# HGRN mixer: the key-by-query products of levels 64 and 32 with stationary tiles of 64 and 32 columns

## Chip, cores and metric

One NeuronCore of a Trainium2 chip. The metric is the device time of one execution in microseconds (us), the median of several runs.

## The reference, cut to what matters

Four sequence-mixing layers follow each other on 512 tokens of 1024 features, in fp32, each with a feed-forward network behind it. The change touches the third, the HGRN mixer with 8 heads of 128 keys and 128 values. For token t and an earlier token s of one head,

```
forget = lower_bound + (1 - lower_bound) * sigmoid(f);  k = 1 - forget;  q = silu(q) / sqrt(128)
scores[t, s] = sum_k q[t, k] * k[s, k] * prod over j in (s, t] of forget[j, k]     (s <= t)
o[t] = sum_s scores[t, s] * v[s]
```

The decay depends on the key feature, so it can't be taken out of the sum over k. The reference walks through chunks of 32 tokens with a state; the kernel computes the same sums otherwise.

## The kernel before

**Weights.** Each 128x1024 slot of weights comes by DMA to `raw`, is rounded to `w_hi` by ScalarE (L1015) and gets its remainder `w_lo` from VectorE (`low_over`, L1492). A dense product is then three fp32r matmuls, L443, L444 and L445, of 128 stationary columns and 512 moving ones; one slot is 24 of them.

**The levels.** `cq` and `ck` hold queries and keys with the features on the partitions and 512 tokens along the free dimension. The scores are built by halving: level 0 has the diagonal, and level m (`LEVELS = (1, 2, 4, 8, 16, 32, 64)`, index `lv - 1`) has the pairs in which the key is in the first half and the query in the second half of the same block of 2m tokens. Between two levels VectorE multiplies queries of second halves (L1972), keys of first halves (L1973) and the products of forget gates (L1974) onward (`decay`). Longer distances than 128 tokens follow after the levels (L884, L888).

TensorE computes a level for four heads e (group g, head 4g + e), in banks 4 to 7 of PSUM. For each of `TT` = 4 tiles of 128 tokens there is one fp32 matmul, L855: all 128 keys of the tile are stationary, and the 64 queries of second halves move. It gives 128 keys x 64 queries, of which a level needs only some. VectorE takes these out with a mask (`keep_level`, L1950, `copy_predicated`): only entries whose key is in the first half of the query's own block are copied to `ca`; all others of the bank are left. The mask `cmask` comes from the host.

**Order of the work.** Each engine's program is written out by hand. TensorE does, in group 0, level 0, then a slot of the value projection, level 1, the next slot, and so on; level 32 (`lv` 6) stands between value slots 5 and 6, and level 64 (`lv` 7) behind value slots 6 and 7. In group 1 each level is followed by a slot of the gate projection: level 32, gate slot 6, level 64, gate slot 7. After level 64 come the products with the values (L872, which waits for `level_kept`, and in group 1 for `g_evac`), then L884, L896, L888 and L900. Each L855 group of a head waits for `upd` (the decays for this level, L846) and for `level_kept` of the level before, and its last matmul raises `level_full`.

VectorE does per level, head by head, `keep_level(g, lv - 1, e)` and `decay(g, lv, e)`; then, in group 1, the gate's evacuation (L1978) and more, and the weights' remainder L1492.

Each fp32 matmul of the program stands in the trace as two pairs of a weight load (PEld LDWEIGHTS) and a MATMUL: L855 has 256 matmuls and 512 pairs. "128*128", "128*64" and "128*32" in the rows are rows and columns of the array that an instruction takes. Two other places of the kernel already use column tiles: L959 and L716 (attention values, 64 columns at partitions 0 or 64, in turns), and L770 (the depthwise convolution, 32 columns at partitions 0, 32, 64 and 96). L716 has seven matmuls a head, three with 256 moving columns and four with 128.

Of the kernel before, what the change touches and what calls it, by code (L numbers as in the profile page):

```python
# [12 lines left out]
P = 128  # L13
# [14 lines left out]
LEVELS = (1, 2, 4, 8, 16, 32, 64)  # L28
# [98 lines left out]
def build(nc, weights, vectors, squares, select_d, masks_d, x_t, out_t):  # L127
    with ExitStack() as ctx:
        def sb(name, shape, dt, where=ctx):
            return where.enter_context(nc.sbuf_tensor(name, shape, dt))  # L130
# [60 lines left out]
        with ExitStack() as hgrn:  # L191
            with ExitStack() as qk:
                cq = sb("cq", [P, HG_HEADS, T], F32, qk)
                ck = sb("ck", [P, HG_HEADS, T], F32, qk)
# [26 lines left out]
        bank = [ctx.enter_context(nc.psum_tensor(f"bank{i}", [P, T], F32)) for i in range(8)]  # L221
# [218 lines left out]
        def _(pe):  # L440
            def product(out, wh, wl, xh, xl, start, stop):

                pe.matmul(out, wh, xh, start=start, stop=False)  # L443
                pe.matmul(out, wh, xl, start=False, stop=False)  # L444
                return pe.matmul(out, wl, xh, start=False, stop=stop)  # L445
# [234 lines left out]
            for k in range(KC):  # L680
                wide = [w[:, k, :, :].rearrange("p r n -> p (r n)") for w in (wf_hi, wf_lo)]
                last = product(bank[4][:, :], *wide, u_hi[:, k, :], u_lo[:, k, :], k == 0, k == KC - 1)
# [120 lines left out]
            def value_slot(n):  # L803
                def free(t):
                    if n == 0:
                        pe.wait_ge(c_evac, 2 * KC)
                    elif n == 4:
                        pe.wait_ge(i_evac, t + 1)
                token_major(SLOT["c_i"] + n, bank, n % 4, n % 4 == 3, free if n in (0, 4) else None)

            def gate_slot(n):
                if n < 2:
                    pe.wait_ge(co_evac, n + 1)
                else:
                    pe.wait_ge(g_evac, n - 1)
                chunk(SLOT["c_g"] + n, 0, bank[n % 2][:, :], u_hi, u_lo)

            def head_square(hd):

                pe.wait_ge(sq_ready, SQ["c_head"] + hd + 1)  # L820
                if hd < 4:
                    pe.wait_ge(co_evac, 4)
                    out = bank[2 + hd % 2]
                else:
                    pe.wait_ge(far_kept, 16)
                    out = bank[hd]
                if hd in (2, 3):
                    pe.wait_ge(rs_ln, RS["c_head"] + hd - 1)
                pe.matmul(out[:, :], ones[:, :], sq[:, hd % 2, :], start=True, stop=True).then_inc(sq_used, 1)
# [3 lines left out]
            for g in range(2):  # L833
                for lv in range(N_LEVEL):
                    last_first = g == 0 and lv == N_LEVEL - 1
                    if last_first:
                        value_slot(lv)
                    for e in range(4):
                        hd = 4 * g + e
                        if lv == 0:  # L840
                            pe.wait_ge(c_qkf, 3 * (hd + 1))
                            if g:
                                pe.wait_ge(far_kept, 8)
                        else:

                            pe.wait_ge(upd, upd_count(g, lv, e))  # L846
                            pe.wait_ge(level_kept, 4 * (N_LEVEL * g + lv - 1) + e + 1)
                        for t in range(TT):
                            s = slice(t * P, (t + 1) * P)
                            if lv == 0:  # L850
                                out, queries = bank[4 + e][:, s], cq[:, hd, s]
                            else:
                                out = bank[4 + e][:, t * P // 2:(t + 1) * P // 2]
                                queries = cq[:, hd, s].rearrange("p (b two s) -> p b two s", two=2, s=LEVELS[lv - 1])[:, :, 1, :]
                            last = pe.matmul(out, ck[:, hd, s], queries, start=True, stop=True)  # L855
                        last.then_inc(level_full, 1)
                    if g:
                        gate_slot(lv)
                    elif not last_first:
                        value_slot(lv)  # L860
                    if g and 1 <= lv <= 4:
                        head_square(lv - 1)

                for e in range(4):
                    hd = 4 * g + e
                    pe.wait_ge(level_kept, 4 * (N_LEVEL * g + N_LEVEL - 1) + e + 1)
                    if g == 0:
                        pe.wait_ge(i_evac, KC)
                    else:
                        pe.wait_ge(g_evac, KC)  # L870
                    for t in range(TT):
                        last = pe.matmul(bank[e][:, t * P:(t + 1) * P], cv[:, t, hd * P:(hd + 1) * P],  # L872
                                         ca[:, e, t * P:(t + 1) * P], start=(t == 0), stop=False, skip_group_check=True)
                    last.then_inc(pv_part, 1)

                for far in range(2):
                    for e in range(4):
                        hd = 4 * g + e
                        pe.wait_ge(upd, upd_count(g, N_LEVEL + far, e))
                        if far:  # L880
                            pe.wait_ge(far_kept, 8 * g + e + 1)
                        if far == 0:
                            for i in range(2):
                                last = pe.matmul(bank[4 + e][:, i * P:(i + 1) * P], ck[:, hd, 2 * i * P:(2 * i + 1) * P],  # L884
                                                 cq[:, hd, (2 * i + 1) * P:(2 * i + 2) * P], start=True, stop=True)
                        else:
                            for i in range(2):
                                last = pe.matmul(bank[4 + e][:, 2 * i * P:2 * (i + 1) * P], ck[:, hd, i * P:(i + 1) * P],  # L888
                                                 cq[:, hd, 2 * P:4 * P], start=True, stop=True)
                        last.then_inc(far_full, 1)  # L890
                    for e in range(4):
                        hd = 4 * g + e
                        pe.wait_ge(far_kept, 8 * g + 4 * far + e + 1)
                        for i in range(2):
                            if far == 0:
                                last = pe.matmul(bank[e][:, (2 * i + 1) * P:(2 * i + 2) * P],  # L896
                                                 cv[:, 2 * i, hd * P:(hd + 1) * P], ca[:, e, i * P:(i + 1) * P],
                                                 start=False, stop=False, skip_group_check=True)
                            else:
                                last = pe.matmul(bank[e][:, 2 * P:4 * P], cv[:, i, hd * P:(hd + 1) * P],  # L900
                                                 ca[:, e, 2 * i * P:2 * (i + 1) * P], start=False, stop=(i == 1),
                                                 skip_group_check=True)
                        last.then_inc(pv_part if far == 0 else co_full, 1)
# [68 lines left out]
            for t in range(TT):  # L972
                last = pe.transpose(bank[0][:, t * P:(t + 1) * P], ut[:, 1, t * P:(t + 1) * P], ident)
# [32 lines left out]
        def _(act):  # L1006
# [69 lines left out]
            def keep(stat, n, src, t):  # L1076

                _, gain, at, _ = BOUNDARY[stat]
                bias = shifted_gain[:, n:n + 1] if stat == "b_post" else 0.0
                act.activation(m[:, n, t], src, ACT.Identity, scale=col(gain, at + n), bias=bias).then_inc(made_ready, 1)  # L1080
# [21 lines left out]
            def half_input(stat, half, chunks):  # L1102

                made, _, _, split = BOUNDARY[stat]
                for c in chunks:
                    act.wait_ge(h_ready, RESID[made] + PAIRS * half + c // 2 + 1)
                    act.activation(u_hi[:, c, tokens(half)], h[:, c, tokens(half)], ACT.Identity, scale=pre_gain(split, c))\
                       .then_inc(uh_ready, 1)
# [1044 lines left out]
def upd_count(g, lv, e):  # L2153

    per_group = 4 + 8 * 12
    before = 0 if lv <= 1 else 4 + 12 * (lv - 2)
    return per_group * g + before + (e + 1 if lv == 1 else 3 * e + 2)
# [83 lines left out]
```

## Time and profile before

| | us |
|---|---|
| median of 3 runs (2430.32 to 2433.72) | 2433.08 |
| the profiled execution | 2434.33 |
| its span, first to last instruction | 2432.5 |

Times in rows are us from the span's start unless ns stands there. "PE" is the matmul part of TensorE and "PEld" its weight loads, which run beside it; DVE is VectorE, ACT ScalarE. Ends of matmuls are modelled. In rows of a timeline, xN says how many instructions of one kind were merged into the row, and a bracket at the end says how long the engine had been idle and what released it.

### The profile page before, as it was taken

The numbers are of one execution on the slowest core, as the hardware profiler recorded it, in microseconds if no ns is written. First come the engines' busy times: TensorE is split into PE (matmuls) and PEld (weight loads), VectorE is DVE, ScalarE is ACT, GpSimd is POOL, SyncE is SP. The second block draws the span as 40 slices with busy tenths as digits, with TensorE's granted clock in tenths as the row PEclk, the third lists the DMA queues.
The fourth block names the chain that finished last, engine by engine and source line by source line (L and its number), as shares of the span: only waits on it lengthen the run. The fifth ranks groups of instructions, "written<-read, shape, count | busy, mean of one in ns | idle before, by whom it ended". The sixth has DMA issues, their size and how long they took to land.

```text
span 2432.5 us, 32810 instructions
## 1 busy us (share of the span) xinstructions
PE 2364.1 (97%) x12314; PEld 1963.0 (81%) x12314; DVE 1313.0 (54%) x2017; ACT 866.8 (36%) x1314; POOL 23.9 (1%) x16
## 2 busy tenths in 40 slices
PE   8999999999898999999999999999999989999997
PEld 6888888889764888888988987888888777888886
DVE  6564655523534564542366585666623895666523
ACT  6444422222423532222342254333322564333322
POOL 0000000000110000000000000000000000000000
PEclk9999999999999999999999999999999999999999
DMA  4112222222362232222222111222222212222222
GB/s 155 61 61 85 80 99 99 95 95 82 93 174 80 70 104 95 95 95 95 87 91 78 44 57 58 96 98 100 95 95 95 72 36 70 104 96 101 97 95 78
DMA packets 68013, 216.30 MB, mean 89 GB/s; under 512 B 11600, under 2 KB 12112, under 8 KB 67920
## 3 DMA queue, kind: packets, MB, share of 16 engines
q1 hardware_dynamic: 67632, 214.63, 26.3%
q8 instruction: 66, 1.08, 0.2%
q10 hardware_dynamic: 288, 0.36, 0.1%
q14 instruction: 27, 0.22, 0.0%
HBM read 210.64 MB, written 4.33 MB: 88 GB/s over the span
## 4 chain that ended last, share of the span: by engine, by line
PE 86%; DVE 7%; ACT 4%; issue 1%; DMA 1%; SPq 0%; DVEq 0%; ACTq 0%
PE bank L443 25%; PE bank L445 24%; PE bank L444 24%; PE bank L855 2%; PE bank L770 2%; PE bank L642 1%; PE bank L641 1%; PE bank L643 1%; DVE w_lo L1492 1%; ACT w_hi L1015 1%; ACT ds L1444 1%; DVE h L1553 1%; DVE m L1548 1%; DVE acc L1521 1%; DVE small L2101 1%
## 5 line engine op out<-in xcount | busy, mean ns | idle before, releaser
L1015 ACT ACTIVATE w_hi<-raw 128x1024 fp32r<-128x1024 f32 x378 | 400.3, 1059 | 1171.4 <-PE bank L445 1043.1
L443 PE MATMUL bank<-u_hi,w_hi 128*128 128x512 f32 (+1 forms) x2088 | 795.5, 381 | 11.1 <-DVE w_lo L1492 4.6
L445 PE MATMUL bank<-u_hi,w_lo 128*128 128x512 f32 (+1 forms) x2088 | 786.8, 377 | 0.0
L444 PE MATMUL bank<-u_lo,w_hi 128*128 128x512 f32 (+1 forms) x2088 | 786.7, 377 | 0.0
L1492 DVE TENSOR_TENSOR w_lo<-raw,w_hi 128x1024 fp32r<-128x1024 f32 x378 | 462.6, 1225 | 413.5 <-ACT w_hi L1015 413.0
L443 PEld LDWEIGHTS bank<-u_hi,w_hi 128*128 128x128 f32 x2088 | 394.3, 189 | 91.4 <-issue 13.1
L445 PEld LDWEIGHTS bank<-u_hi,w_lo 128*128 128x128 f32 x2088 | 393.8, 189 | 72.4
L444 PEld LDWEIGHTS bank<-u_lo,w_hi 128*128 128x128 f32 x2088 | 394.5, 189 | 71.4 <-issue 1.2
L443 PE MATMUL bank<-hid_hi,w_hi 128*128 (+1 forms) x528 | 208.0, 394 | 0.0
L445 PE MATMUL bank<-hid_hi,w_lo 128*128 (+1 forms) x528 | 207.0, 392 | 0.0
L444 PE MATMUL bank<-hid_lo,w_hi 128*128 (+1 forms) x528 | 204.9, 388 | 0.0
L1646 DVE TENSOR_TENSOR ut<-gconv,bank 128x512 f32<-128x512 f32 x88 | 60.5, 688 | 157.3 <-PE bank L445 149.8
L445 PEld LDWEIGHTS bank<-hid_hi,w_lo 128*128 128x128 f32 x528 | 99.1, 188 | 23.2
L444 PEld LDWEIGHTS bank<-hid_lo,w_hi 128*128 128x128 f32 x528 | 99.1, 188 | 22.2
L443 PEld LDWEIGHTS bank<-hid_hi,w_hi 128*128 128x128 f32 x528 | 99.3, 188 | 19.7
L641 PE MATMUL bank<-hid_hi,w_hi 128*128 128x256 f32 x352 | 98.6, 280 | 0.0
L642 PE MATMUL bank<-hid_lo,w_hi 128*128 128x256 f32 x352 | 98.6, 280 | 0.0
L643 PE MATMUL bank<-hid_hi,w_lo 128*128 128x256 f32 x352 | 98.2, 279 | 0.0
L1640 DVE SCALAR_TENSOR_TENSOR gconv<-ut,vec,gconv 128x511 f32<-128x511 f32 x88 | 66.1, 751 | 56.6 <-ACT gconv L1164 50.6
L1167 ACT ACTIVATE gconv<-gconv 128x512 f32<-128x512 f32 x88 | 55.0, 625 | 88.7 <-DVE gconv L1640 76.8
L1653 DVE TENSOR_TENSOR hid_lo<-ut,hid_hi 128x512 f32 (+1 forms) x88 | 61.0, 693 | 10.1
L641 PEld LDWEIGHTS bank<-hid_hi,w_hi 128*128 128x128 f32 x352 | 66.2, 188 | 0.1
(287 smaller groups left out, 2590.4 us busy)
## 6 DMA issues: line engine op xcount, KB each, us to landing
raw<-weights_dram SPq DMA_DIRECT2D x378, 512.0 KB, 3.2
bz<-gated_dram SPq DMA_DIRECT2D x32, 270.0 KB, 4.9
gated_dram<-bz SPq DMA_DIRECT2D x8, 272.0 KB, 2.1
h<-x_t_dram SPq DMA_DIRECT2D x8, 256.0 KB, 6.6
out_dram<-m SPq DMA_DIRECT2D x8, 256.0 KB, 2.2
ap<-select_dram SPq DMA_DIRECT2D x1, 512.0 KB, 8.7
vec<-vectors_dram SPq DMA_DIRECT2D x1, 343.0 KB, 7.6
cmask<-masks_dram ACTq DMA_DIRECT2D x1, 224.0 KB, 2.6
```

Source lines behind the costliest of these rows:

```text
L443: pe.matmul(out, wh, xh, start=start, stop=False)
L444: pe.matmul(out, wh, xl, start=False, stop=False)
L445: return pe.matmul(out, wl, xh, start=False, stop=stop)
L641: pe.matmul(out, ws[0], xh, start=first, stop=False, skip_group_check=True)
L642: pe.matmul(out, ws[0], xl, start=False, stop=False, skip_group_check=True)
L643: last = pe.matmul(out, ws[1], xh, start=False, stop=final, skip_group_check=True)
L1015: act.activation(w_hi[:, j, :], raw[:, j, :], ACT.Copy).then_inc(hi_ready, 1)
L1167: act.activation(gconv[:, b, :], gconv[:, b, :], ACT.Silu).then_inc(gate_ready, 1)
L1492: dve.tensor_tensor(w_lo[:, j, :], raw[:, j, :], w_hi[:, j, :].bitcast(F32), ALU.subtract).then_inc(w_ready, 1)
L1640: dve.scalar_tensor_tensor(out=gconv[:, b, back:], in0=ut[:, b, 0:T - back], scalar=w, in1=gconv[:, b, back:], op0=ALU.mult, op1=ALU.add). ...
L1646: dve.tensor_tensor(ut[:, b, :], gconv[:, b, :], bank[2 * b + 1][:, :], ALU.mult).then_inc(ht_ready, 1)
L1653: dve.tensor_tensor(lo, ut[:, b, :], hi.bitcast(F32), ALU.subtract).then_inc(hid_ready, 1)
```

## The change

For level 32 and level 64 only (`lv` 6 and 7) L855 is replaced. Per tile of 128 tokens, level 64 is one matmul with the 64 keys of the first half stationary and the 64 queries of the second half moving, written to partitions 0 to 63 of the bank. Level 32 is two matmuls per tile, each with the 32 keys of one block's first half and the 32 queries of its second half: one to partitions 0 to 31 and 32 columns of the bank, one to partitions 64 to 95 and the next 32 columns. Level 64 keeps its number of matmuls, level 32 has twice as many. The semaphores, the masks and the other engines' programs are unchanged; parts of the bank that are no longer written are not copied by the mask.

```
                         for t in range(TT):
                             s = slice(t * P, (t + 1) * P)
+                            if lv and LEVELS[lv - 1] >= 32:
+
+                                mm = LEVELS[lv - 1]
+                                for at in range(0, P, 2 * mm):
+                                    to = slice(t * P // 2 + at // 2, t * P // 2 + at // 2 + mm)
+                                    last = pe.matmul(bank[4 + e][at:at + mm, to], ck[:, hd, t * P + at:t * P + at + mm],
+                                                     cq[:, hd, t * P + at + mm:t * P + at + 2 * mm], start=True, stop=True)
+                                continue
                             if lv == 0:
                                 out, queries = bank[4 + e][:, s], cq[:, hd, s]
                             else:
```

## Rows read from the trace of the kernel before

**Rows 1.** The page: busy time of each engine, and the chain that ended last.

```profile
PE 2364.1 (97%) x12314; PEld 1963.0 (81%) x12314; DVE 1313.0 (54%) x2017; ACT 866.8 (36%) x1314; POOL 23.9 (1%) x16
...
PE 86%; DVE 7%; ACT 4%; issue 1%; DMA 1%; SPq 0%; DVEq 0%; ACTq 0%
```

**Rows 2.** The chain through the HGRN stage: start, us on the chain, what.

```profile
1358.65 3.52 PE bank L855 x32
1362.17 0.29 PE bank L443
...
1363.38 0.23 PE bank L445
...
1373.13 3.52 PE bank L855 x32
1376.65 3.63 PE bank L872 x32
...
1448.45 3.52 PE bank L855 x32
...
1457.50 3.52 PE bank L855 x32
1461.02 0.29 PE bank L443
```

**Rows 3.** Stretches of the HGRN stage: busy us of PE, PEld, DVE, ACT, POOL; then the granted clock.

```profile
1440.00:1460.00 20.00, 20.00 (x132) 18.07 (x131) 16.32 (x43) 9.37 (x11) 0.00 (x0) 1.00 0.21 71
```

**Rows 4.** Groups by line and shape: count, busy us, mean ns of one.

```profile
L855 PEld LDWEIGHTS bank<-cq,ck 128*128 128x128 f32 x512 | 59.6, 192 | 2.8 <-issue 1.7 <-DVE ct L1974 0.2
L770 PEld LDWEIGHTS bank<-bz,bw 128*32 128x32 f32 x512 | 16.4, 110 | 37.7 <-issue 37.7
...
L959 PEld LDWEIGHTS bank<-dpt,dv 128*64 128x64 f32 x224 | 12.1, 137 | 1.5 <-issue 0.7
...
L959 PE MATMUL bank<-dpt,dv 128*64 128x128 f32 x224 | 14.0, 276 | 0.0
```

**Rows 5.** Timeline of TensorE at the column-tiled places L959 and L770.

```profile
1940.98 1.75 PE L959 MATMUL bank<-dpt,dv 128*64 128x128 f32 x28
...
661.10 0.15 PEld L770 LDWEIGHTS bank<-bz,bw 128*32 128x32 f32 x4 [0.27 <-issue]
661.52 0.16 PEld L770 LDWEIGHTS bank<-bz,bw 128*32 128x32 f32 x4 [0.27 <-issue]
...
660.67 7.07 PE L770 MATMUL bank<-bz,bw 128*32 128x512 f32 x64 [0.78 <-DMA bz<-gated_dram]
```

**Rows 6.** The chain around column-tiled blocks, each with the dense matmul behind it.

```profile
192.78 1.23 PE bank L716 x12
194.01 0.43 PE bank L443
...
2018.66 1.68 PE bank L959 x28
2020.34 0.43 PE bank L443
```

**Rows 7.** VectorE beside levels 32 and 64, and TensorE's L872, in order of time.

```profile
1374.01 0.45 DVE L1950 COPY_PREDICATED ca<-cmask,bank 128x256 f32<-128x256 uint32 x1 [8.94 <-PE bank L855]
...
1376.49 3.79 PE L872 MATMUL bank<-ca,cv 128*128 128x128 f32 x32
...
1377.24 0.44 DVE L1950 COPY_PREDICATED ca<-cmask,bank 128x256 f32<-128x256 uint32 x1
...
1448.29 3.68 PE L855 MATMUL bank<-cq,ck 128*128 128x64 f32 x32
...
1448.88 0.43 DVE L1973 TENSOR_TENSOR ck<-ck,ct 128x256 f32<-128x256 f32 x1
...
1457.54 0.69 DVE L1978 TENSOR_TENSOR cg<-bank,rs 128x512 f32<-128x512 f32 x1 [1.49 <-PE bank L445]
...
1466.59 0.69 DVE L1978 TENSOR_TENSOR cg<-bank,rs 128x512 f32<-128x512 f32 x1 [2.43 <-PE bank L445]
```

## The prediction

> **What bounds the kernel now.** I read the page first: TensorE is busy 97% of the span and carries 86% of the chain that ended last [rows 1]. The average can hide stages with another limit, so the next view is the chain inside the HGRN stage. There every level is a piece of L855, 32 pairs in 3.52 us, with dense matmuls directly before and behind it; the four blocks that the change touches (level 32 and level 64 of both groups) are four such pieces [rows 2]. So a microsecond taken from one of these blocks is a microsecond of the end, as long as no other engine becomes late. The granted clock there is 1.00, the upper of its two levels, 2.4 GHz [rows 3]; TensorE has no idle time in that stretch.
>
> What bounds one block? 3.52 us over 32 pairs is 110 ns a pair [rows 2]. The weight loads tell why. One takes 192 ns with 128 columns, 137 with 64, 110 with 32 [rows 4]: 0.85 ns a column, (192 - 110) / 96, above a fixed part of about 83 ns. 128 columns are thus 109 ns of loading proper, the pitch of the pairs; the fixed part overlaps. What moves is cheaper: L959 has 28 pairs with 128 moving columns in 1.75 us [rows 5]; taking off the duration of the last, 0.276 [rows 4], leaves 1.47 / 27 = 55 ns a pair, with two column tiles working side by side. On one tile that is 110 ns for 128 columns, 0.85 ns a column. L770 agrees: its bursts of four start 0.42 us apart, one load for each of four tiles, so 512 columns take 0.42 us on a tile, 0.82 ns a column [rows 5]. I use 0.84. The 64 queries of L855 hence need only 54 ns, and the block waits for the loads. These are what the change shortens.
>
> **The change part by part.** Removed are four blocks of L855. Each costs 3.52 us on the chain and 0.06 more behind it, since the first dense matmul afterwards holds 0.29 us where one in the stream holds 0.23 [rows 2]. That makes 3.58 us a block.
>
> Entering and leaving a column-tiled mode has a price, which two places show. L959: 28 pairs at 128 x 0.84 / 2 = 54 ns are 1.51 us, the chain holds 1.68, and the dense matmul behind it holds 0.43 in place of 0.23: 0.17 + 0.20 = 0.37 us. L716: three matmuls of 256 and four of 128 columns are 1280 columns, two pairs each, on two tiles: 1280 x 0.84 = 1.08 us; the chain holds 1.23, and again 0.43 behind: 0.15 + 0.20 = 0.35 us [rows 6, 2]. I take 0.37 for each new block. It is paid four times, because dense work in 128 columns lies between the blocks; 0.06 of it is what the old block pays too, and that is already in the 3.58.
>
> Level 64, two blocks of 32 pairs. The load has 64 columns, 55 ns; 64 columns move, 54 ns. All lie on one column tile (partitions 0 to 63), so nothing runs beside them on another, but load and movement overlap on one tile in L855 already: 110 ns a pair, not 109 + 54 [rows 2]. Estimate 55 ns: 32 x 0.055 + 0.37 = 2.13 us. Gain 3.58 - 2.13 = 1.45 us a block.
>
> Level 32, two blocks of 64 pairs, twice as many. The load has 32 columns, 27 ns; 32 columns move, 27 ns. No row has so short a pair in a long row of them, so I bound it. From above: 55 ns, the shortest sustained pitch in the trace, L959's [rows 5]; then a block is 64 x 0.055 + 0.37 = 3.89 us and loses 0.31. From below: 14 ns, if the two tiles (partitions 0 and 64) work fully side by side. That so many can be issued is shown by L770's bursts, whose four loads take 0.15 to 0.16 us in all and so stand (0.155 - 0.110) / 3 = 15 ns apart [rows 5, 4]; a block is then 64 x 0.014 + 0.37 = 1.27 us and gains 2.31. I take 28 ns, the column sum on one tile without help from the second, because L855's pitch too lies within 1 ns of its column sum, and because the 15 ns are a burst and no steady stream. A block: 64 x 0.028 + 0.37 = 2.16 us, gain 1.42.
>
> A rule of the Trainium skill speaks against this step. "TensorEngine Tiling (Array Packing)", section Instruction Overhead, says that a matmul on this chip carries about 60 cycles, so that very few moving columns cost the same as 60. No row here shows a matmul so short. If its cycles are those of 2.4 GHz and count once for each MATMUL record, that is an estimated 25 ns, below 28, and the sum stays. If they count for each of the two fp32 passes inside a record, it is 50 ns, level 32 costs 3.57 us and the whole change gains 2.9 us. That second reading is the first rival below.
>
> **Sum.** 2 x 1.45 + 2 x 1.42 = 5.7 us. The profiled execution took 2434.33 us with a span of 2432.5, 1.8 us outside it and 1.3 above the median of the runs. The same difference applied to the median: 2433.08 - 5.7 = 2427.4 us, or 0.24% faster.
>
> **What must keep up.** VectorE's operations are unchanged (a copy with a mask goes over all 256 columns whatever was written), so it still takes (1377.24 - 1374.01) / 3 = 1.08 us a head. Three places matter [rows 7]. After level 64 of group 0, L872 waits for the kept scores. The fourth head's is ready at 1377.24 + 0.44 = 1377.68 and would come some 0.3 earlier, with the first head's level; TensorE wants it at about 1376.49 + 2.72 = 1379.21, in future 1.45 earlier, 1377.76. Cover left: 0.4 us. In level 32 of group 1, the fourth head's keys are decayed at 1448.88 + 0.43 = 1449.31, and L855 wants them at 1448.29 + 2.64 = 1450.9; with 16 pairs of 28 ns a head and 0.15 of entry it wants them at 1449.8. Cover left: 0.5 us; at 14 ns a pair it would be gone and TensorE would wait 0.2. In group 1 VectorE has been idle 1.49 us when gate slot 6 ends, and 2.43 us when slot 7 ends; a gain of 1.4 just before each uses most of the first, not all of the second. So all work of VectorE stays hidden; if a cover is gone, the loss is what exceeds it, tenths of a microsecond. The weights for later slots start earlier together with the slots that free their buffers, and DMA's share is 0.21 in this stretch [rows 3].
>
> **Rivals.**
>
> *A floor under short pairs* (the pair of 32 columns costs what one of 64 does). For it: no sustained pitch under 55 ns stands in the trace. Against it: 55 is also what L959's columns need, so that row shows no floor. Time: gain 2 x (1.45 - 0.31) = 2.3 us, 2430.8 us, within 0.2%. A floor of about 35 ns, between the two, gives 64 x 0.035 + 0.37 = 2.61, a gain of 0.97 each and 4.8 in all: 2428.3, the boundary of what can be told.
>
> *The two tiles of level 32 work side by side.* For it: L959 and L770 do so. 2 x (1.45 + 2.31) = 7.5 us, less a few tenths for VectorE: 2425.8 us, faster.
>
> *Load and movement on one narrow tile don't overlap.* Level 64 would cost 109 ns a pair, 3.86 us; level 32, 54 ns, 3.83 us. The gains turn into losses of 0.28 and 0.25, 1.1 us in all: 2434.1 us, the same. Against it: L959's pairs come in twos on one tile and still reach 55 ns.
>
> *The other sign: the fixed part of the load becomes exposed in column tiles.* In a mode of few columns each load would have to be complete before its matmul and the next load: 137 ns a pair in level 64 (4.75 us a block) and 110 ns in level 32 (7.41 us). Loss 2 x (1.17 + 3.83) = 10.0 us: 2443.1 us. It decides for slower once the mean pair costs more than 92 ns, where 2 x (96 p + 0.74) exceeds the old 14.3 us by 4.9. Against it: L959 and L716 hide that part.
>
> **Chances.** What a measurement can tell from no change is about 0.2%, 4.9 us, so the forecast lies only just beyond that. Forecast (28 ns, or up to 35) 0.36; tiles side by side 0.16; a floor from 35 to 55 ns 0.34; no overlap, or a cover of VectorE gone so that most of the gain is given back, 0.08; slower 0.06. Faster: 0.52, same: 0.42, slower: 0.06. The predicted time is the forecast's, 2427.4. The range reaches from 2425.0 (the side-by-side case, with the runs' own spread of more than 1 us) to 2432.2 (the floor at 55 ns with the same spread); the forecast's own range is 2426 to 2428.5.
>
> **What would show it.** In the chain, level 64 should be a piece of 32 pairs at 1.8 to 2.1 us and level 32 one of 64 pairs at about 2; the dense matmul behind each should hold 0.43. The loads should last 137 and 110 ns. A level-32 block of 3.5 us or more is the floor; one near 1.3 is the two tiles. A new wait of L872 or L855 for VectorE would show a cover that is gone. The prediction is wrong if the pitch at 32 columns lies far from 28 ns, if the mode's entry costs more where both neighbours are in 128 columns, or if some later stage gives the time back by a wait that it doesn't have now.

## The result and the profile after

| | before | after |
|---|---|---|
| median of 8 runs, us | 2432.76 (2430.32 to 2436.56) | 2426.84 (2423.57 to 2428.24) |
| ratio, 95% interval | | 0.9971 (0.9962 to 0.9981) |
| span of the profiled execution, us | 2432.5 | 2426.0 |
| the HGRN stage in it, us | 177.36 | 170.98 |

The change is 0.29% faster; 2427.4 was predicted. A second measurement of the same kernel gave 0.9975 (0.9964 to 0.9986) and a median of 2425.31 us, 7 runs.

The "HGRN stage" here is the time from the first weight load of level 0 to the first load of L829 behind both groups. Two rows of the timeline of TensorE's weight loads mark it; first those of the kernel before, then those of the kernel after with its new blocks:

```profile
1303.98 3.76 PEld L855 LDWEIGHTS bank<-cq,ck 128*128 128x128 f32 x32
...
1481.34 0.41 PEld L829 LDWEIGHTS bank<-sq,ones 128*128 128x128 f32 x2
```

```profile
1304.28 3.76 PEld L863 LDWEIGHTS bank<-cq,ck 128*128 128x128 f32 x32
...
1358.88 1.09 PEld L855 LDWEIGHTS bank<-cq,ck 128*32 128x32 f32 x64 [0.35 <-issue]
...
1371.12 1.94 PEld L855 LDWEIGHTS bank<-cq,ck 128*64 128x64 f32 x32 [0.35 <-issue]
...
1475.26 0.41 PEld L829 LDWEIGHTS bank<-sq,ones 128*128 128x128 f32 x2
```

In the new kernel L855 is the narrow matmul only; the wide one of levels 0 to 16 is L863, and lines behind it are 8 higher (L872 is now L880, ScalarE's evacuation of the value slots L1358). Level 32 is the row of 64 pairs: 1.09 us less one load of 0.112 over 63 steps is 15.5 ns a pair. Level 64: (1.94 - 0.138) / 31 = 58 ns a pair.

The chain through the same stage, to be read against [rows 2]:

```profile
1358.95 1.14 PE bank L855 x64
1360.08 0.43 PE bank L443
...
1371.25 0.56 issue
1371.81 1.84 ACT cv L1358 x3
1373.79 3.81 PE bank L880 x32
...
1445.77 0.88 PE bank L855 x48
1446.67 0.45 PE bank L855 x16
1447.12 0.43 PE bank L443
...
1452.80 2.01 PE bank L855 x32
1454.81 0.43 PE bank L443
```

Each old block cost 3.58 us. Level 32 of group 0 now costs 1.14 and 0.20 more behind it (0.43 in place of 0.23): gain 2.24. Level 32 of group 1 stands in two pieces, 1.35 us with a wait between, plus 0.20: gain 2.03. Level 64 of group 1 costs 2.01 + 0.20: gain 1.37. Level 64 of group 0 has dropped out of the chain: L880 begins 2.59 us after the end of the last dense matmul on the chain (1371.20), where L872 began 3.52 after it, but what lies between is now ScalarE. That is 0.93, of which L880 gives 0.18 back (3.81 on the chain, before 3.63; why is not shown, and in group 1 the piece held 3.81 before as well). The sum is 6.39 us, and the stage is 6.38 shorter. Three rows in the view of waits are new:

```profile
PE bank L880 <- ACT cv L1358: 0.6, 1, 0.6
...
PEld bank L880 <- DVE ca L1958: 0.7, 1, 0.7
...
PEld bank L855 <- DVE ct L1982: 0.4, 1, 0.4
```

(us in total, times, longest). The first two are one wait, of L880's matmuls and of its loads: VectorE's copy for the first head, which the second row names, had ended at 1372.27, 1.5 us before L880 began. The third is level 32 of group 1.

Outside the stage nothing of the program changed, and yet it is where the spread lies: a second profile of the same kernel has 170.97 us in the stage and a span 3.6 us shorter. The record shows what goes with it. In the stage the granted clock is 1.00 in both profiles; outside it falls to 0.50 for some microseconds here and there, and not in the same places each time. Between 620 and 640 us, for example, its mean is 0.83 in the first profile and 1.00 in the second. Over the whole span it is 0.991 in the first and 0.994 in the second. Of the eight runs of the change, the four with a mean clock of 0.991 took 2427.34 to 2428.24 us and the four with 0.993 took 2423.57 to 2426.34. So below, an experiment is read first by its stage, which repeated to 0.01 us in the one kernel profiled twice, and by medians only where the difference is large.

### The profile page after: what moved, and what is told of

Its sections match the earlier page's. It is cut to its first block, busy times and chain, and to the rows that moved or that the text cites. A ratio compares the mean times of both kernels' runs of the same rounds, so it can differ in the third digit from the quotient of the medians.

```text
span 2426.0 us, 32938 instructions
## 1 busy us (share of the span) xinstructions
PE 2358.9 (97%) x12378; PEld 1956.4 (81%) x12378; DVE 1313.0 (54%) x2017; ACT 866.9 (36%) x1314; POOL 23.1 (1%) x16
## 4 chain that ended last, share of the span: by engine, by line
PE 86%; DVE 7%; ACT 4%; issue 1%; DMA 1%; SPq 0%; DVEq 0%; ACTq 0%
PE bank L443 25%; PE bank L445 24%; PE bank L444 24%; PE bank L770 2%; PE bank L863 2%; PE bank L642 1%; PE bank L641 1%; PE bank L643 1%; DVE w_lo L1500 1%; ACT w_hi L1023 1%; ACT ds L1452 1%; DVE h L1561 1%; DVE m L1556 1%; DVE acc L1529 1%; DVE small L2109 1%
```

## The experiments

The stage is read as above. The last three kernels with strips also have the wait per bank.

| kernel | stage, us | median, us (runs) | ratio to before, 95% |
|---|---|---|---|
| before | 177.36 | 2432.76 (8) | |
| after | 170.98 | 2426.84 (8) | 0.9971 (0.9962 to 0.9981) |
| level 64 alone | 175.22 | 2429.45 (11) | 0.9984 (0.9975 to 0.9994) |
| level 32 alone | 173.09 | 2427.47 (10) | 0.9978 (0.9968 to 0.9987) |
| wait per bank | 170.33 | 2426.72 (10) | 0.9973 (0.9964 to 0.9983) |
| level 32 on one tile | 172.76 | 2427.71 (1) | |
| level 64 on two tiles | 170.03 | 2422.52 (1) | |
| level 64, heads 0 and 1 narrow | 172.03 | 2425.66 (1) | |
| level 64, heads 0 and 2 narrow | 172.62 | 2428.49 (1) | |
| strips of 32 keys | 159.43 | 2416.76 (5) | 0.9933 (0.9919 to 0.9947) |
| strips and wait per bank | 160.39 | 2416.88 (5) | 0.9933 (0.9919 to 0.9946) |
| strips in group 0, wait per bank | 160.11 | 2416.56 (5) | 0.9929 (0.9916 to 0.9943) |
| strips in group 0 and level 1 of group 1, wait per bank | 158.84 | 2411.54 (4) | 0.9908 (0.9893 to 0.9924) |

### Each level alone

```
-                            if lv and LEVELS[lv - 1] >= 32:
+                            if lv and LEVELS[lv - 1] == 64:
```

> Only level 64 uses the narrow tile; level 32 stays at 128 columns. In the trace of the changed kernel a level-64 block is 32 pairs in 2.01 us on the chain with 0.43 for the dense matmul behind, 2.21 us in all against 3.58 before: 1.37 us of gain in group 1. In group 0, L880 waited for ScalarE's evacuation of the last value slot (0.59 us idle), which leaves 0.98. Theory: the two levels' gains add, and this kernel gains 1.37 + 0.98 = 2.35 us on the kernel before. Rival (the wait for ScalarE is only there because level 32's gain makes everything earlier): 2.7 us, and no idle time before the products with the values in group 0.

The stage is 2.14 us shorter than before, against 2.35 expected by the theory; the same 0.59 us of waiting for ScalarE stands before L880. So that wait comes from the narrow level 64, and the rival is out. Of the 0.21 missing, 0.18 are what L880 gives back (3.81 in place of 3.63), and the 0.98 of the expectation should have been 0.93.

With `== 32` in the same line:

> Only level 32 uses narrow tiles. In the changed kernel its block is 64 pairs in 1.14 us plus 0.20 behind in group 0 (gain 2.24) and 1.35 plus 0.20 in group 1, where it waited for VectorE's decay of the fourth head (gain 2.03). Theory: this kernel gains 4.2 to 4.3 us, more than half of the whole change. Rival (what level 32 gains is lost again later, since VectorE or ScalarE become late): under 3.5 us.

4.27 us shorter. Together 2.14 + 4.27 = 6.41, the 6.38 of the change: the two parts add. Two thirds of the gain are level 32's, the part that I had sized by a guess between far bounds.

### The wait behind level 64 in group 0

```
                     if g == 0:
-                        pe.wait_ge(i_evac, KC)
+                        pe.wait_ge(i_evac, TT + e + 1)
```

> The changed kernel, with one wait made finer: in group 0 the products with the values wait, for head e, until bank e alone has been evacuated by ScalarE (count TT + e + 1), and not until all four banks have. Theory (the 0.6 us of idle time before them is this wait for ScalarE): the idle time falls to under 0.1, they start 0.4 to 0.6 us earlier after the last dense matmul, and the kernel gains about 0.4 us on the changed kernel, which is too little for the medians and is read from the chain. Rival (it was VectorE's kept scores that came last, ScalarE only by name): the idle time stays.

The chain of this kernel there:

```profile
1368.26 2.01 PE bank L855 x32
1370.27 3.77 PE bank L880 x32
```

The narrow level 64 is on the chain again and L880 starts as its last pair ends. The stage is 0.65 us shorter than the change's, 0.4 had been expected; the medians can't tell. The new wait was that for ScalarE's four evacuations of the last value slot, which take 2.42 us from the end of the last dense matmul, while L855 is now done 2.4 us after that matmul's start, in place of 3.9. A head writes its products to one bank, and needs only that one to be free; the values that it reads in group 0 come from the first four slots.

### Why a pair of level 32 costs 15.5 ns

```
-                                    last = pe.matmul(bank[4 + e][at:at + mm, to], ck[:, hd, t * P + at:t * P + at + mm],
+                                    last = pe.matmul(bank[4 + e][0:mm, to], ck[:, hd, t * P + at:t * P + at + mm],
```

> The changed kernel, but level 32 writes both of a tile's products to partitions 0 to 31, so that all 64 pairs of a block lie on one column tile (the products of the second block land on the wrong partitions; everything else is as in the change). Theory (the pitch is the time of the 32-column load, 27 ns, shared by the tiles that take turns, plus some 2 ns): 15.5 ns a pair becomes 28 to 30 ns, and a block's loads take about 1.9 us in place of 1.09. Rival (the pitch of 15.5 ns is the rate at which pairs are issued, whatever the tile): it stays at 15 to 16 ns.

```profile
1357.65 2.10 PEld L855 LDWEIGHTS bank<-cq,ck 128*32 128x32 f32 x64 [0.35 <-issue]
```

(2.10 - 0.112) / 63 = 31.6 ns a pair, twice the 15.5 of the change, with the same number of the same pairs. On one tile it is the tile that sets the pace. Whether 15.5 ns is two tiles' share of it or a limit of issue just above, this kernel can't tell; the 8.9 ns on four tiles below can, and they rule the limit out. The chain has the block of this kernel as

```profile
1357.72 2.14 PE bank L855 x64
```

The other way round, level 64 on two tiles:

```
+                                    row = 64 * (t % 2) if mm == 64 else at
-                                    last = pe.matmul(bank[4 + e][at:at + mm, to], ck[:, hd, t * P + at:t * P + at + mm],
+                                    last = pe.matmul(bank[4 + e][row:row + mm, to], ck[:, hd, t * P + at:t * P + at + mm],
```

> The changed kernel, but level 64 writes every second tile's product to partitions 64 to 127 (so these land on the wrong partitions). The 32 pairs of a block then lie on two column tiles in turns. Theory (load time shared by the tiles): 58 ns a pair becomes 29 to 31 ns, and a block's loads take about 1.05 us in place of 1.94. Rival (64 columns are loaded over one path, one load after the other, whatever the tile): it stays at 55 to 58 ns.

```profile
1366.72 1.01 PEld L856 LDWEIGHTS bank<-cq,ck 128*64 128x64 f32 x32 [0.35 <-issue]
```

(1.01 - 0.138) / 31 = 28 ns a pair in place of 58. In both, column tiles that take turns share the time. Whether that is the time of loading or of moving, levels 64 and 32 can't tell, since as many columns move as are loaded.

### The price of the narrow mode

```
-                            if lv and LEVELS[lv - 1] >= 32:
+                            if lv and (LEVELS[lv - 1] == 32 or LEVELS[lv - 1] == 64 and e in (0, 1)):
```

> The changed kernel, but in level 64 only heads 0 and 1 of each group use the narrow tile and heads 2 and 3 the 128-column one. One entry into the narrow mode and one exit a block. Theory (a switch costs about 0.35 us for both ways, besides the pairs): 16 pairs at 58 ns, 16 at 110 and 0.35, 3.0 us from dense matmul to dense matmul.

> The same work as with heads 0 and 1 narrow, but heads 0 and 2 are narrow and 1 and 3 wide, so that a block enters and leaves the narrow mode twice. Theory (each pair of switches costs about 0.35 us, also between two fp32 blocks): its level-64 block is 0.3 to 0.4 us longer than that with heads 0 and 1 narrow. Rival (the 0.35 us belong to the border with the fp32r matmuls, not to the mode): the two blocks are equal within 0.1 us.

The chains through level 64 of group 1, first with heads 0 and 1 narrow, then with heads 0 and 2 (L855 narrow, L863 wide):

```profile
1450.45 1.08 PE bank L855 x16
1451.52 1.93 PE bank L863 x16
1453.45 0.29 PE bank L443
```

```profile
1452.96 0.61 PE bank L855 x8
1453.57 1.03 PE bank L863 x8
1454.61 0.61 PE bank L855 x8
1455.21 1.03 PE bank L863 x8
1456.25 0.28 PE bank L443
```

3.00 us from dense matmul to dense matmul against 3.29: one more entry and exit costs 0.29 us, and the two stages differ by 0.59 for two blocks. The price is the mode's, also between two fp32 blocks, and a little lower there than the 0.35 that the change's blocks show.

### Strips of 32 keys in all levels

If tiles share the time, four of them should do better than two. Levels 1 to 16 can be cut into strips of 32 tokens, since their pairs never cross one; the mask already drops the rest.

```
+                            if lv:
+                                step = 32
...
+                                        wide = step
+                                        queries = cq[:, hd, t * P + at:t * P + at + step]\
+                                            .rearrange("p (b two s) -> p b two s", two=2, s=LEVELS[lv - 1])[:, :, 1, :]
+                                        to = slice(t * P // 2 + at // 2, t * P // 2 + at // 2 + step // 2)
+                                    last = pe.matmul(bank[4 + e][at:at + wide, to], ck[:, hd, t * P + at:t * P + at + wide],
+                                                     queries, start=True, stop=True)
```

> The change carried on to levels 1 to 16: for each tile of 128 tokens, four matmuls whose stationary operand is a strip of 32 keys and whose moving operand is the strip's 16 queries of second halves, written to partitions 0, 32, 64 and 96. 128 pairs a block in place of 32. Levels 32 and 64 as in the change. Theory (a pair with a narrow tile costs 15.5 ns, whatever its columns, as long as neighbouring pairs lie on other tiles): a block is 128 x 0.0155 = 2.0 us plus 0.35 for entry and exit, 2.35 against 3.58, so ten blocks gain 12 us more, 2414 us, minus what TensorE then waits for VectorE, which is up to 18 of 20 us busy in group 1: 2414 to 2419 us. Rival 1 (pairs have a floor between 25 and 30 ns when so many follow each other): blocks of 3.5 to 4.2 us, and no gain or a loss of a few us against the change. Rival 2 (VectorE is the bound as soon as the blocks are shorter): long waits of L855 and of the dense slots for VectorE, and less than half of the 12 us.

Its weight loads in group 0 and, below, in group 1, head by head (L861 is the narrow matmul):

```profile
1320.98 1.25 PEld L861 LDWEIGHTS bank<-cq,ck 128*32 128x32 f32 x128 [0.35 <-DVE ck L1987]
1334.87 1.24 PEld L861 LDWEIGHTS bank<-cq,ck 128*32 128x32 f32 x128 [0.35 <-issue]
...
1404.52 0.35 PEld L861 LDWEIGHTS bank<-cq,ck 128*32 128x32 f32 x32 [1.07 <-DVE ck L1987]
1405.94 0.35 PEld L861 LDWEIGHTS bank<-cq,ck 128*32 128x32 f32 x32 [1.07 <-DVE ck L1987]
```

A block of 128 pairs takes (1.24 - 0.11) / 127 = 8.9 ns a pair, not the 15.5 of the theory: four tiles, not two. Here 32 columns are loaded and 16 move. At 0.85 and 0.84 ns a column, shared by four, the loads would need an estimated 6.8 ns a pair and the movement 3.4, so the loads are the longer of the two; what the other 2 ns are is open. Ten blocks could have gained some 20 us; the stage is 11.55 us shorter than the change's. Group 0 gave 10.2 of these (from level 0 to level 64's first load 56.61 us, in the change 66.84), group 1 only 1.3. There TensorE waits for VectorE's decay before most heads, in level 4 up to 1.07 us for 0.35 us of work, and something else happens behind it. Stretches of 1 us; the columns are the stretch's length, busy us of PE, PEld, DVE, ACT and POOL with their counts, the granted clock, DMA's share and GB/s:

```profile
1403.00:1404.00 1.00, 0.55 (x50) 0.39 (x37) 1.00 (x4) 1.00 (x1) 0.00 (x0) 1.00 0.79 279
1404.00:1405.00 1.00, 0.45 (x32) 0.35 (x32) 1.00 (x4) 0.20 (x1) 0.00 (x0) 1.00 0.62 242
1405.00:1406.00 1.00, 0.06 (x5) 0.06 (x9) 1.00 (x4) 0.00 (x0) 0.00 (x0) 1.00 0.00 0
1406.00:1407.00 1.00, 1.00 (x35) 0.88 (x36) 1.00 (x3) 0.00 (x0) 0.00 (x0) 0.94 0.00 0
1407.00:1408.00 1.00, 1.00 (x4) 0.81 (x3) 1.00 (x2) 0.66 (x2) 0.00 (x0) 0.50 0.00 0
1408.00:1409.00 1.00, 1.00 (x3) 0.74 (x3) 1.00 (x2) 1.00 (x1) 0.00 (x0) 0.50 0.00 0
1409.00:1410.00 1.00, 1.00 (x4) 0.78 (x3) 0.09 (x1) 0.96 (x3) 0.00 (x0) 0.50 0.00 0
```

After three stretches in which TensorE was busy 0.55, 0.45 and 0.06 us, the granted clock is 0.50, 1.2 GHz, for some 3.4 us of dense matmuls. Neither theory nor rivals had this; that VectorE is the bound in group 1 was the second rival.

```
-                        pe.wait_ge(i_evac, KC)
+                        pe.wait_ge(i_evac, TT + e + 1)
```

> The kernel with strips of 32 keys in levels 1 to 16, together with the wait per bank before the products with the values in group 0. Theory: the two add, since they lie in different places: 0.5 us less than with the strips alone, some 2416 us, and 0.7% below the kernel before.

This failed: the stage is 0.96 us longer, not 0.5 shorter. The wait itself worked as before: from level 64's first load to L886, the products with the values of this kernel, 2.01 us in place of 2.64. But the clock fell in another place, behind level 32 of group 1 (columns as above):

```profile
1435.00:1436.00 1.00, 0.45 (x16) 0.33 (x16) 1.00 (x5) 0.39 (x1) 0.00 (x0) 1.00 0.87 340
1436.00:1437.00 1.00, 0.47 (x16) 0.42 (x16) 1.00 (x4) 0.00 (x0) 0.00 (x0) 0.84 0.10 41
1437.00:1438.00 1.00, 1.00 (x6) 0.83 (x3) 1.00 (x3) 0.20 (x1) 0.00 (x0) 0.50 0.00 0
```

There the time from the last load group of level 32 to level 64 is 7.60 us, in the strips kernel 6.04: 1.56 longer. In the strips kernel the fall lay behind level 4. It made the next sums (L829) 0.59 us later there, but from these sums to the last head of level 32 that kernel took 0.64 less, since this stretch waits for VectorE and ScalarE anyway: that fall cost nothing in the end. Which of the weak stretches brings the clock down was not controlled. The same blocks of level 4, with the same waits of 1.07 us, stand in this kernel too, and the clock stayed at 1.00 behind them.

So the last two kernels, both with the wait per bank, keep the wide matmuls where TensorE waits for VectorE anyhow: they lose no time there and fill it.

```
-                            if lv:
+                            if lv and (g == 0 or lv >= 6):
```

> Strips of 32 keys in levels 1 to 16 of group 0 only, group 1 as in the change, and the wait per bank. In the strips kernel group 0 gained 10.2 us on the change and group 1 1.3, and in group 1 TensorE stood waiting for VectorE between short blocks, behind which the granted clock fell to 0.50 for some 3.4 us. Theory (VectorE bounds group 1 and the lower clock takes part of what is left): the stage from level 0 to the first sums of squares takes 170.98 - 10.23 - 0.6 = 160.2 us, with a granted clock of 1.00 throughout, 1 us or less above the strips kernel's 159.43. Rival (group 1's strips matter more than their trace says, since the fall of the clock is not caused by them): the clock falls here too, and the stage is over 161 us.

The stage takes 160.11 us, as expected (160.2), and the granted clock is 1.00 in all of it. Then `(g == 0 or lv == 1 or lv >= 6)`:

> The same with level 1 of group 1 in strips as well, where VectorE comes from a pause and TensorE has work before and behind. Theory: one more block gains up to 2 us, the clock stays at 1.00, and the stage takes 158.2 to 159.5 us, the shortest so far. Rival (VectorE has no slack anywhere in group 1): the stage is equal to that with group 0 alone within 0.3 us, since the next level waits for VectorE as long as level 1 was shortened.

Stretches of 60 us of this kernel, columns as above:

```profile
1340.00:1400.00 60.00, 60.00 (x531) 51.83 (x530) 39.54 (x103) 20.92 (x31) 0.00 (x0) 1.00 0.16 53
1400.00:1460.00 60.00, 58.46 (x414) 50.40 (x413) 45.59 (x123) 32.12 (x41) 0.00 (x0) 1.00 0.17 54
```

158.84 us, the shortest stage, 1.27 below strips in group 0 alone, with the clock at 1.00. It uses fewer narrow matmuls than the strips kernel, and its stage is 0.59 us shorter; but it has the wait per bank, which is worth 0.65 by itself. The fair neighbour is the kernel with strips in all levels and that wait: 160.39 us, and an estimated 158.8 without the 1.56 of its fall of the clock. So narrow matmuls in levels 2 to 16 of group 1 gain nothing, and lose only if the clock falls where it costs.

The median of this kernel, 2411.54 us in 4 runs, is 0.92% below the 2435.00 of the kernel before beside it. From the kernel with group 0 alone its median is 5.0 us away and its stage 1.3. The rest goes with the clock outside the stage: three of the five runs of the kernel with group 0 alone had a mean clock of 0.991 (2416.56 to 2419.67 us), its two with 0.994 took 2411.16 and 2414.44, and the four of this kernel had 0.992 or 0.993.

The changed kernel once more, beside the strips:

> The changed kernel itself, beside the strips on the same chip: 6 to 7 us below the kernel before, 9 to 10 us above the strips.

It came out 7.1 us below the kernel before and 8.4 above the strips with the wait per bank, both just outside what was expected.

## Why the prediction was right, and where it was not

**What bounds.** Right. The four blocks lay on the chain and the stage shrank by what they shrank, less two waits.

**Entry and exit, 0.37 us a block.** Right: 2.01 + 0.20 - 32 x 0.058 = 0.35, and 1.14 + 0.20 - 64 x 0.0155 = 0.35. The Trainium skill says in "TensorEngine Tiling (Array Packing)", Key Properties, that a change of tiling mode drains TensorE. The traces agree that a change has a price, 0.29 to 0.35 us for both ways; that it is a drain, none of them shows.

**Level 64, 55 ns a pair and 2.13 us a block.** Right within 0.1: 58 ns and 2.21 us. Load and movement do overlap on one tile; that rival is out, as is the one by which the fixed part of the load becomes exposed (137 and 110 ns a pair).

**Level 32, 28 ns a pair.** This term was mis-sized. The pairs take 15.5 ns, near the lower bound of 14 that I had, and a block 1.34 us, not 2.16. The step that failed is "the column sum on one tile without help from the second". The kernel with one tile shows what I had priced: its pairs take 31.6 ns, and its block holds 2.14 us on the chain and 0.20 behind. My reason for distrusting the 15 ns of L770's bursts, that they are no steady stream, was empty: 128 pairs in a row keep 8.9 ns. The rival of tiles working side by side, to which I gave 0.16, is what happened.

**The floor.** Out. The rule of the Trainium skill that I cited ("TensorEngine Tiling (Array Packing)", Instruction Overhead) would, by the estimates in the prediction, have made a pair 50 ns in its second reading and 25 in its first. The pairs stood 15.5 and 8.9 ns apart, so neither reading bounds pairs on alternating tiles. The Trainium skill also says, in "TensorE: Matmul & The Clock Gate", Part 1, that starts never come closer than about 25 ns. These rows contradict it for matmuls on alternating column tiles; on one tile, with 31.6 ns, no run here does.

**What must keep up.** Half right. For VectorE in level 32 of group 1 I had said that the cover ends at 14 ns a pair and TensorE would wait 0.2; at 15.5 ns group 1's block gained 0.21 less than group 0's, with the wait in the trace. For L872 in group 0 I looked at VectorE alone and called the cover 0.4 us. The instruction also waits for `i_evac`, and ScalarE's evacuation had been hidden by level 64 itself. It cost about 0.6 us, as the wait per bank shows (0.65). I had named that wait's neighbour in group 1, `g_evac`, and not asked what ended last on the other branch.

**The sum.** 5.7 us predicted, 6.4 in the stage: 0.82 a block too little on level 32 (less 0.2 for VectorE in one), 0.08 a block too much on level 64, and 0.62 lost in group 0 by ScalarE (0.44) and L880's longer piece (0.18). The errors partly cancel, so the hit of the median by 0.6 us says less than it seems to. The other sign's mechanism had no part in it.

## What to carry to other kernels

A short fp32 matmul whose time is its weight load gets cheaper by the columns that it doesn't load, and once more by the number of column tiles that take turns: place consecutive matmuls on different partitions, and pay 0.29 to 0.35 us for each visit to the narrow mode. Before shortening a block, list every semaphore that the next instruction waits for and which engine was hidden by the block. And where TensorE then waits for another engine in small pieces, leave the longer matmuls in: the shorter ones gained nothing here, and the granted clock fell behind them in both kernels that had them (why there and not behind other such blocks is open).

## What the runs showed of the hardware

- Time of a pair of weight load and matmul, fp32, equal or fewer moving columns: 110 ns with 128 columns; 58 ns with 64 on one tile and 28 on two; 31.6 ns with 32 on one tile, 15.5 on two, 8.9 on four. That is 0.85 ns a loaded column, divided by the tiles, plus 1 to 4.4 ns. Only the rows with 128 columns (64 moving) and with four tiles (16 moving) tell loading from movement.
- The granted clock fell from 1.00 to 0.50 for some 3.4 us behind a run of short narrow blocks with waits between them, in both kernels that had all levels of group 1 in strips, and in neither of the two that had not.
- The same kernel's span differed by 3.6 us between two profiled executions, none of it in the stage of 171 us. The mean granted clock was 0.991 in the longer and 0.994 in the shorter, and 1.00 within the stage in both.
